# Stick-breaking heads: both minima formed on VectorE before the logarithm lands, one of two subtractions moved to GpSimd

## The reference, cut to what matters

```
z = einsum('bhqc,bhkc->bhqk', q_blk, kt) * scale
log_stay = where(causal, log_sigmoid(-z), 0.0)
later = cumsum(log_stay, axis=3, reverse=True) - log_stay
attn = where(causal, exp(log_sigmoid(z) + later), 0.0)
o = einsum('bhqk,bhkc->bhqc', attn, vt)
```

## Time and profile before

| | us |
|---|---|
| median of three runs | 2757.64 (2757.19 to 2757.9) |
| the profiled execution | 2757.27 |
| its span | 2755.3 |
| PE busy | 2718.4 (99% of the span) |
| DVE busy | 1537.2 (56%) |
| ACT busy | 1110.5 (40%) |
| POOL busy | 40.8 (1%) |

### The profile page before, as it was taken

How to read it: one execution, slowest core, us unless ns; L and a number is a source line. 1 busy time by engine, 2 the same in 40 slices (tenths; PEclk the granted TensorE clock), 3 DMA queues, 4 the chain that set the end, 5 groups by cost and what they waited for, 6 DMA issues and landing times.

```text
span 2755.3 us, 33598 instructions
## 1 busy us (share of the span) xinstructions
PE 2718.4 (99%) x12697; PEld 2228.6 (81%) x12697; DVE 1537.2 (56%) x2107; ACT 1110.5 (40%) x1516; POOL 40.8 (1%) x36
## 2 busy tenths in 40 slices
PE   8999999999999999999999999999999999999998
PEld 7887788888888778888888888888878678788887
DVE  5376855456635685554567664434564556644344
ACT  3246544334313654532352443323343654532223
POOL 3000000000200000000000000000000000000000
PEclk9999999999999999999999999999999999999999
DMA  5322233332332123333243423333343123233322
GB/s 163 92 62 61 84 94 94 95 101 84 105 106 71 53 62 107 91 95 103 80 122 92 116 84 92 95 103 91 91 108 85 48 70 123 77 92 91 107 80 88
DMA packets 466510, 252.02 MB, mean 91 GB/s; under 512 B 22670, under 2 KB 460903, under 8 KB 466287
## 3 DMA queue, kind: packets, MB, share of 16 engines
q1 hardware_dynamic: 466415, 250.70, 31.6%
HBM read 248.54 MB, written 2.11 MB: 91 GB/s over the span
## 4 chain that ended last, share of the span: by engine, by line
PE 91%; DVE 5%; ACT 3%; issue 1%; DMA 0%; ACTq 0%; SPq 0%; DVEq 0%
PE M L750 26%; PE M L752 26%; PE M L751 26%; DVE w_lo L2139 1%; PE M L838 1%; PE M L836 1%; PE M L837 1%; PE A L935 1%; PE A L910 1%; PE A L982 1%; PE A L924 0%; PE A L750 0%; PE A L752 0%; PE A L751 0%; DVE prob L2593 0%
## 5 line engine op out<-in xcount | busy, mean ns | idle before, releaser
L750 PE MATMUL M<-h_hi,w_hi 128*128 128x512 f32 x2184 | 859.6, 394 | 0.8 <-issue 0.7
L752 PE MATMUL M<-h_hi,w_lo 128*128 128x512 f32 x2184 | 850.2, 389 | 0.0
L751 PE MATMUL M<-h_lo,w_hi 128*128 128x512 f32 x2184 | 850.1, 389 | 0.0
L1519 ACT ACTIVATE w_hi<-stage 128x1024 fp32r<-128x1024 f32 (+3 forms) x504 | 497.1, 1026 | 714.2 <-PE M L752 589.4
L2139 DVE TENSOR_TENSOR w_lo<-stage,w_hi 128x1024 fp32r<-128x1024 f32 (+3 forms) x504 | 589.6, 1205 | 165.2 <-ACT w_hi L1519 164.5
L750 PEld LDWEIGHTS M<-h_hi,w_hi 128*128 128x128 f32 x2184 | 409.9, 188 | 89.8 <-issue 3.9
L752 PEld LDWEIGHTS M<-h_hi,w_lo 128*128 128x128 f32 x2184 | 409.8, 188 | 86.5
L751 PEld LDWEIGHTS M<-h_lo,w_hi 128*128 128x128 f32 x2184 | 410.0, 188 | 85.8 <-issue 2.6
L750 PE MATMUL M<-hid_hi,w_hi 128*128 128x512 f32 x704 | 274.8, 390 | 0.2 <-DVE w_lo L2139 0.2
L752 PE MATMUL M<-hid_hi,w_lo 128*128 128x512 f32 x704 | 274.0, 389 | 0.0
L751 PE MATMUL M<-hid_lo,w_hi 128*128 128x512 f32 x704 | 273.9, 389 | 0.0
(11 more groups left out here) (488 smaller groups left out, 3214.0 us busy)
## 6 DMA issues: line engine op xcount, KB each, us to landing
stage<-in_w_up SPq DMA_DIRECT2D x88, 512.0 KB, 4.4
stage<-in_ffn_w_gate_up SPq DMA_DIRECT2D x88, 512.0 KB, 4.5
stage<-in_w_in SPq DMA_DIRECT2D x80, 512.0 KB, 4.6
stage<-in_w_down SPq DMA_DIRECT2D x32, 384.0 KB, 3.7
stage<-in_ffn_w_down SPq DMA_DIRECT2D x32, 384.0 KB, 3.6
stage<-in_od_w_in SPq DMA_DIRECT2D x21, 512.0 KB, 3.9
stage<-in_w_down SPq DMA_DIRECT2D x32, 320.0 KB, 3.3
stage<-in_ffn_w_down SPq DMA_DIRECT2D x32, 320.0 KB, 3.3
```

What stands on the lines that cost most here:

```text
L750: pe.matmul(bank, a_hi, b_hi, start=(n == 0), stop=False)
L751: pe.matmul(bank, a_hi, b_lo, start=False, stop=False)
L752: last = pe.matmul(bank, a_lo, b_hi, start=False, stop=(n == k - 1))
L1519: act.activation(w_hi[:, s, part * HALF:part * HALF + n], stage[:, part, 0:n], ACT.Copy)\
```

## The change

On DVE both minima are now formed from the banks before the wait for the logarithm: `log_sig` = min(z, 0) in three instructions and `log_stay` = min(-z, 0) in three more. After the logarithm DVE subtracts L from `log_stay` only, and goes on to the diagonals. L is subtracted from `log_sig` by GpSimd, which waits for the same logarithm; DVE waits for GpSimd ahead of the addition of the running sums. GpSimd's semaphore counts its copies and these subtractions together, so PE's wait for the copies is given another count.

```diff
-        perm_done = sem("perm_done")
+        pool_done = sem("pool_done")
+        def pool_steps(l):
+            return l * (2 * KT + SLOTS)
...
-                pe.wait_ge(perm_done, (l + 1) * 2 * KT)
+                pe.wait_ge(pool_done, pool_steps(l) + 2 * KT)
...
+                for h in range(SLOTS):
+                    n = l * SLOTS + h
+                    pool.wait_ge(st_dve, 4 * n + 1)
+                    pool.wait_ge(log_done, n + 1)
+                    pool.tensor_tensor(log_sig, log_sig, log_ones[h % 3], ALU.subtract).then_inc(pool_done, 1)
...
                 last.then_inc(st_dve, 1)
-                dve.wait_ge(st_dve, 4 * n + 1)
+                for bank, at, width in parts:
+                    last = dve.tensor_scalar(log_stay[:, at:at + width], bank[:, 0:width], -scale, 0.0, ALU.mult, ALU.min)
+                last.then_inc(st_dve, 1)
+                dve.wait_ge(st_dve, 4 * n + 2)
                 dve.wait_ge(log_done, n + 1)
-                dve.tensor_tensor(log_sig, log_sig, log_one, ALU.subtract).then_inc(st_dve, 1)
-                dve.wait_ge(st_dve, 4 * n + 2)
-                for bank, at, width in parts:
-                    last = dve.scalar_tensor_tensor(log_stay[:, at:at + width], bank[:, 0:width], -scale,
-                                                    log_sig[:, at:at + width], ALU.mult, ALU.add)
-                last.then_inc(st_dve, 1)
+                dve.tensor_tensor(log_stay, log_stay, log_one, ALU.subtract).then_inc(st_dve, 1)
                 dve.wait_ge(st_dve, 4 * n + 3)
...
                 gate_split(l, SLOTS + h - 1)
+                dve.wait_ge(pool_done, pool_steps(l) + 2 * KT + h + 1)
                 dve.wait_ge(later_done, n + 1)
```

More of the change, by code:

```diff
@@ L1505, in _ @@
                     pool.wait_ge(h_lo_done, split_norm(2 * l) + k + 1)
-                    pool.tensor_copy(as_residue(hp_hi[:, k, :], 1), by_residue(h_hi[:, k, :], 1)).then_inc(perm_done, 1)
-                    pool.tensor_copy(as_residue(hp_lo[:, k, :], 1), by_residue(h_lo[:, k, :], 1)).then_inc(perm_done, 1)
+                    pool.tensor_copy(as_residue(hp_hi[:, k, :], 1), by_residue(h_hi[:, k, :], 1)).then_inc(pool_done, 1)
+                    pool.tensor_copy(as_residue(hp_lo[:, k, :], 1), by_residue(h_lo[:, k, :], 1)).then_inc(pool_done, 1)
+                for h in range(SLOTS):
[3 more added lines that the diff above has]
+                    pool.tensor_tensor(log_sig, log_sig, log_ones[h % 3], ALU.subtract).then_inc(pool_done, 1)
         @block.scalar
```

## The result

The changed kernel takes 2768.14 us (median of six runs, 2764.06 to 2770.0), the kernel before 2757.41 beside it: ratio 1.0033, 95% interval 1.0023 to 1.0042, or 9 us slower (6 to 12). A later set of runs gave 2768.53 and a ratio of 1.0036 (1.0022 to 1.0049), with a second profile.

The account below looks back on a forecast made before the run. PE, busy 99% of the span, was taken as the bound, so only its waits matter. Late `stay_hi` costs 3.55 us a layer, 7.1 in two; on 2757.27 that gives 2764.4, stated as 2764.5, range 2753 to 2770.

Parts of the forecast that it names:

- The minima hidden ahead of the logarithm: Three minima moved into DVE's idle 1.73 us before it subtracts: 1.62 us, fitting with 0.1 to spare, taken as costing nothing.
- POOL's instruction ahead of the masks: After the logarithm, POOL's subtraction goes in before DVE's masks, which end after 5.11 us against 4.06.
- rival A: The forecast itself: POOL's subtraction holds DVE up before `stay_hi`, 7.1 us in two layers; chance 0.70.
- Rival B: DVE keeps its turn through subtraction and masks, POOL works after them: 2 us gained, 2755.5; chance 0.16, with mixtures.
- The hold of 2.7 us: POOL's subtraction of 1280 columns, priced from its 1.09 us cast of 512 columns; bounds 0 to 5.4 us.
- `stay_hi` late by 1.05: In each head, POOL's hold of 2.70 less the 1.65 us step removed behind the logarithm delays `stay_hi` by 1.05 us.
- PE's loss of 3.55 us a layer: PE's added waiting in heads 0 to 3 of a layer: 1.05, 1.0, 0.45 and 1.05 us, 7.1 in two layers.
- the prediction's formula: PE's loss in a layer's stick heads for a lateness D over 0.6 us: 4 D - 0.65.
- DVE's new wait on POOL: Ahead of line 2445, the addition of the sums: costs nothing unless POOL takes over 7 us.
- PE's renumbered wait: PE's wait for the copies also counts four subtractions that were over long before: costs nothing.

Follow-up runs that it names:

- both edits to DVE: Against the kernel before: minima ahead of the logarithm, both subtractions on DVE, and the second `w_lo` instruction behind the addition of the sums; 2752.35 us, ratio 0.9975.

## Why the prediction was right

The direction, the mechanism and the place held. Forecast 2764.5 in a range of 2753 to 2770; measured 2768.14. (The prediction's own terms, 2757.27 + 7.1 + 0.4, make 2764.8.) Against the kernel before, run beside it, that is 9 us (6 to 12), where 7.1 were forecast, and one term was missing.

- *The minima hidden ahead of the logarithm:* right. 0.2 us were to spare, where 0.1 was estimated, and the run without GpSimd's subtraction shows them free.
- *POOL's instruction ahead of the masks* (rival A): right in every head. DVE came first, POOL waited and went in ahead of four queued short instructions. Rival B, in which the masks pass first, did not occur by itself; made by hand it gives a ratio of 0.9997 (0.9988 to 1.0007) and 0.5 us in the two layers of its profile, where 2 us of gain were worked out.
- *The hold of 2.7 us* from a cast of 512 columns: 2.80 behind DVE's subtraction and 2.96 alone. The 2.8 worked out from the Trainium skill ("GPSIMD Engine Reference", "Performance versus the Vector engine") was the closer; this case now has its own row.
- *`stay_hi` late by 1.05:* 0.97, with the longer hold. The first mask, which was waiting, ends 0.16 after POOL does, where it takes 0.28 alone.
- *PE's loss of 3.55 us a layer:* the prediction's formula gives 3.23 for 0.97, and PE's timeline shows 3.21 before any drop of the clock. Head by head it is 0.98, 0.95, 0.29 and 0.97, where 1.05, 1.0, 0.45 and 1.05 were forecast; head 2, with its slack, lost little. PE's waits for `stay_hi` in the first layer are 2.52, 0.79, none and 1.42, where 2.6, 1.0, 0 and 1.5 were forecast.
- *What was missing from the sum:* the granted clock, which the prediction put at nothing without a word. It carried PE's extra idle time as the whole cost. In the first profile the three drops add 3.6 us to the 6.4 of the late masks; over the runs it is 2 to 3 us beside 6.7. The run with the same lateness and no POOL has drops too. That the forecast of 2764.5 was not further off is in part luck: the lateness was taken 0.08 us too long in each head, which made up for some of it.
- *DVE's new wait on POOL, PE's renumbered wait:* nothing, as said. DVE's line 2453 follows `w_lo` at once in head 0, and no wait of PE on POOL is in the profile.

## What to carry to other kernels

Before a step is given to GpSimd because it is idle, list which instructions of VectorE that read two SBUF tensors fall under it: each of them stands still until GpSimd is done, a mask of 128 columns as much as one of 1280. The move pays only if GpSimd's hold is shorter than what is taken off VectorE's path; here it was 2.8 us against 1.65. (It should also pay where the hold lies under VectorE's instructions that read PSUM, but no run here had room for that.) Cutting GpSimd's work in two did not help: VectorE got one short instruction through in between. And a chain is to be followed to the point where it closes: the work that was left between `stay_lo` and the sums decided whether the earlier `stay_hi` gave a ratio of 0.9986 or of 0.9975.

## What the runs showed of the hardware

- **Who waits for whom.** Against POOL's instruction DVE's with two SBUF operands waits (2.92 for a mask of 0.28; 3.05 for a `stay_lo` of 1.49), and POOL's waits against DVE's (4.25 for a subtraction of 2.96); a DVE instruction with an operand in SBUF and one in PSUM does not wait (1.28 for two, as ever).
- **The lock.** The Trainium skill has this in "SBUF — State Buffer", section "SBUF: two separate sides", as an exclusive lock between GpSimd's instructions and VectorE's with two SBUF inputs, held for the whole instruction by whichever started first. The traces agree, by the durations above.
- **Who goes next.** In the changed kernel the waiting POOL instruction goes in ahead of the first mask in all eight heads, although the mask is queued right behind DVE's subtraction. With POOL's work in two instructions the first mask goes in between them, again in all eight. So the one that waits has the next turn. One row is different: the instruction at 745.32 waited 6.07 us, until five casts of POOL had gone by. What was different there is open.
- **The granted clock.** In the stick heads each drop is about 3.4 us at 1.2 GHz (two came in a row in the layer with `EARLY` changed) and came after PE had waited, but no rule follows from these profiles. In the kernel before, head 0 waits 1.54 in both layers with no drop; with only the `w_lo` moved, a wait of 1.55 in layer 1 is followed by one. With GpSimd after the masks there are waits of 1.76 and no drop; with both subtractions on DVE the longest is 1.7, total idle is less, and there are three drops' worth. What decides is open. What is shown is this: every profile in which `stay_hi` was a microsecond later has at least one drop in each layer's stick heads (five profiles), and those without GpSimd's subtraction, with half of it, with it after the masks, and with both edits to DVE have none.
- **The noise.** The kernel before ranges from 2754.6 to 2763.3 over 28 runs of one set. Most of that goes with the clock: over the 63 runs with a clock on record, 0.001 of mean clock is 1.8 us of time. One drop of 1.7 us is 0.0006 of the span and costs 1.0 to 1.6 us in the stick heads; their number changes from run to run (the two profiles of the changed kernel show three and four there, and outside them the profile without GpSimd's subtraction has lost 8.5 us of clock near 2200 us, the one with it after the masks nothing).
